# RWKV-7 inside a two-block fp32 network: the group norm's root and inverse on four columns per pair instead of 256, spread back through the tensor engine

## The reference, cut to what matters

```
y  = y - mean(y over the 64 channels of the head)
y  = y / sqrt(mean(y * y over the head) + 64e-5) * rw_lnx_g + rw_lnx_b
out = ((y + bonus) * gate) @ rw_wo
```

## Time and profile before

| | |
|---|---|
| median of 3 runs | 2728.96 us (2728.11 to 2732.6) |
| the profiled execution, its own time | 2738.52 us |
| its span, first to last instruction | 2737.0 us |
| busy, share of the span: PE, PEld, DVE, ACT, POOL | 96%, 84%, 76%, 59%, 8% |
| mean granted TensorE clock | 0.985 of full speed |
| the four RWKV units lie at | about 791 to 1004 us |
| the RWKV tail lies at | about 1004 to 1018 us |

### The profile page before, as it was taken

One profiled execution on the slowest core, in us unless ns is written; L12 is line 12 of the kernel. 1 busy time (PEld: TensorE's weight loads), 2 busy tenths in 40 slices (PEclk: granted clock), 3 DMA queues, 4 the chain that ended last, 5 costly groups with the idle time before them and its releaser, 6 DMA issues.

```text
span 2737.0 us, 43598 instructions
## 1 busy us (share of the span) xinstructions
PE 2635.5 (96%) x17668; PEld 2290.9 (84%) x17668; DVE 2068.2 (76%) x2973; ACT 1614.9 (59%) x2394; POOL 226.1 (8%) x229
## 2 busy tenths in 40 slices
PE   8999899999899999999999898999999999999997
PEld 7989789899787779998899896888888888888886
DVE  6667776776744557668655686999999999999995
ACT  5556455555332235543555535877787778778785
POOL 1102000000011117011600010000000000000000
PEclk9999999999999999999999999999999999999999
DMA  7553245455331125543355433999999999899992
GB/s 272 185 185 110 106 169 185 172 183 185 113 106 67 66 92 185 185 166 116 135 186 185 145 130 122 378 351 349 352 375 351 349 351 366 335 364 363 352 375 82
DMA packets 84605, 604.91 MB, mean 221 GB/s; under 512 B 9400, under 2 KB 9528, under 8 KB 12016
## 3 DMA queue, kind: packets, MB, share of 16 engines
q1 hardware_dynamic: 82016, 594.05, 58.9%
q10 hardware_dynamic: 2032, 4.85, 0.5%
q0 software_dynamic: 352, 3.15, 0.3%
HBM read 600.96 MB, written 1.05 MB: 220 GB/s over the span
## 4 chain that ended last, share of the span: by engine, by line
PE 88%; DVE 9%; ACT 2%; issue 1%; DMA 1%; ACTq 0%; DVEq 0%
PE bank L428 86%; DVE arena L2266 2%; DVE weights_lo L418 2%; PE bank L2856 1%; DVE arena L1200 1%; ACT weights_hi L410 1%; DVE rstd L479 1%; DMA x_T<-in_x 0%; DVE x_T L734 0%; DVE arena L2289 0%; DVE arena L555 0%; DVE arena L1202 0%; ACT x_T L546 0%; DVE arena L2980 0%; PE bank L1869 0%
## 5 line engine op out<-in xcount | busy, mean ns | idle before, releaser
L418 DVE TENSOR_TENSOR weights_lo<-raw_weights,weights_hi 128x1024 fp32r<-128x1024 f32 x816 | 1004.1, 1249 | 389.5 <-ACT weights_hi L410 383.9
L410 ACT CAST weights_hi<-raw_weights 128x1024 fp32r<-128x1024 f32 x816 | 849.5, 1050 | 333.4 <-PE bank L428 319.1
L428 PE MATMUL bank<-source,weights_hi 128*128 128x512 f32 (+1 forms) x3040 | 876.7, 356 | 43.0 <-DVE weights_lo L418 18.2
L428 PE MATMUL bank<-source,weights_lo 128*128 128x256 f32 x2400 | 682.2, 284 | 0.0
L428 PEld LDWEIGHTS bank<-source,weights_hi 128*128 128x128 f32 x3040 | 541.8, 194 | 130.6 <-issue 28.0
L428 PEld LDWEIGHTS bank<-source,weights_lo 128*128 128x128 f32 x2400 | 463.2, 193 | 0.1
L418 DVE TENSOR_TENSOR weights_lo<-arena,weights_hi 128x1024 fp32r<-128x1024 f32 x278 | 336.5, 1225 | 32.0 <-ACT weights_hi L410 28.5
L410 ACT CAST weights_hi<-arena 128x1024 fp32r<-128x1024 f32 x278 | 292.2, 1053 | 56.5 <-PE bank L428 40.3
L428 PE MATMUL bank<-weights_hi,source 128*128 128x512 f32 (+1 forms) x1024 | 309.6, 386 | 3.4 <-issue 2.8
L428 PE MATMUL bank<-hidden_hi,weights_hi 128*128 128x256 f32 x912 | 258.3, 283 | 0.0
L428 PE MATMUL bank<-hidden_lo,weights_hi 128*128 128x256 f32 x912 | 258.1, 283 | 0.0
(11 more groups left out here) (317 smaller groups left out, 3387.0 us busy)
## 6 DMA issues: line engine op xcount, KB each, us to landing
raw_weights<-in_exp_in SPq DMA_DIRECT2D x134, 1024.0 KB, 5.4
arena<-in_exp_in SPq DMA_DIRECT2D x90, 1024.0 KB, 5.4
raw_weights<-in_exp_w SPq DMA_DIRECT2D x67, 1024.0 KB, 5.3
arena<-in_exp_w SPq DMA_DIRECT2D x45, 1024.0 KB, 5.6
raw_weights<-in_ffn_w_down SPq DMA_DIRECT2D x44, 1024.0 KB, 5.0
raw_weights<-in_ffn_w_up SPq DMA_DIRECT2D x43, 1024.0 KB, 5.0
raw_weights<-in_ffn_w_gate SPq DMA_DIRECT2D x42, 1024.0 KB, 4.9
raw_weights<-in_dense_w SPq DMA_DIRECT2D x33, 1024.0 KB, 4.9
```

The costliest lines, as they stand in the source:

```text
L410: k.act.copy(k.weights(j)[0], raw_half(k, j)).then_inc(k.w_hi_ready, 1)
L418: k.dve.tensor_tensor(lo, raw_half(k, j), hi.bitcast(F32), ALU.subtract).then_inc(k.w_ready, 1)
L428: return k.pe.matmul(dst, lhsT, rhs, start=start, stop=stop, skip_group_check=shared)
```

## The change

The second head sum no longer fills 128 x 256 with every head's sum repeated over its 64 channels. The squares become the stationary operand, and two columns of `head_ones` the moving one, so that the sum comes out by tokens: 128 tokens x 2 heads, for two token tiles, four columns per pair. The root and the reciprocal work on these four columns. VectorE copies the inverse over 64 columns each into `z.y2` (128 x 256, tokens on the partitions), and TensorE turns it back into channels by tokens with products of `z.y2` and the identity (`spread_tensor`: two per slot, four per unit). The scaling reads the result from PSUM. `spread` becomes a use of banks 4 to 7 for units 0 to 2, and the finish of a unit has one step more: reciprocal and copy at round 2, nothing at 4, scaling at 6, bonus at 8, gate at 10.

```diff
@@ RwkvTiles
+        self.group = [[k.arena[:, at + 8 * i + 4 * j:at + 8 * i + 4 * (j + 1)] for j in range(2)] for i in range(PAIRS)]
@@ the list of bank uses
 for _u in range(1, UNITS):
-    RW_USES += [("K", _u), ("bonus", _u - 1), ("turn", _u - 1)] + [("gate", _c) for _c in range(4) if _u == 1]
+    RW_USES += [("K", _u), ("bonus", _u - 1), ("turn", _u - 1)]
+    RW_USES += [("gate", _c) for _c in range(4)] if _u == 1 else [("spread", _u - 2)]
     RW_USES += [("R", _u), ("norm", _u), ("inv", _u), ("V", _u)]
-RW_USES += [("bonus", UNITS - 1), ("turn", UNITS - 1)] + [("wo", _u) for _u in range(4)]
+RW_USES += [("bonus", UNITS - 1), ("turn", UNITS - 1), ("spread", UNITS - 2)] + [("wo", _u) for _u in range(4)]
+SPREAD_AFTER, SPREAD_ROUND, LAST_SPREAD_AFTER = 12, 5, 7
@@ claim_bank
+        elif earlier[0] == "spread":
+            k.pe.wait_ge(*k.pair_fin[PAIRS - 1].at((PAIRS * earlier[1] + PAIRS - 1, "y_scaled")))
@@ new
+def spread_bank(k, p, slot):
+
+    if p == UNITS - 1:
+        return k.bank[2 * slot + 1][:, 0:T]
+    return use_bank(k, ("spread", p))[:, slot * T:(slot + 1) * T]
+
+
+def spread_tensor(k, t, p):
+
+    if p < UNITS - 1:
+        claim_bank(k, ("spread", p))
+    for i in range(PAIRS):
+        z = PairTiles(k, t, PAIRS * p + i, i)
+        k.pe.wait_ge(*k.pair_fin[i].at((z.kt, "spread")))
+        for s in range(TT):
+            ins = mm(k, spread_bank(k, p, i)[:, s * P:(s + 1) * P], z.y2[:, s * P:(s + 1) * P], k.con("ident"), True, True)
+    ins.then_inc(*k.rw_mm.step(("spread", p)))
@@ dense_tensor
     if u < UNITS:
+        if p > 0:
+            yield from steps(keys, SPREAD_AFTER - 4)
+            spread_tensor(k, t, p - 1)
+            yield
         yield from keys
...
     else:
-        for v in range(4):
-            yield from wo_tensor(k, t, v, range(0, KT - 2 * PAIRS))
+        first = wo_early_tensor(k, t)
+        yield from steps(first, LAST_SPREAD_AFTER)
+        spread_tensor(k, t, p - 1)
+        yield
+        yield from first
@@ rwkv_tensor
-            for _ in range(count + (4 if p == 0 and n in GATE_ROUNDS else 0)):
-                next(dense, None)
+            more = (4 if n in GATE_ROUNDS else 0) if p == 0 else (1 if n == SPREAD_ROUND else 0)
+            for _ in range(count + more):
+                next(dense)
...
     for blocks in (range(KT - 2 * PAIRS, KT - PAIRS), range(KT - PAIRS, KT)):
         for v in range(4):
             for _ in wo_tensor(k, t, v, blocks):
                 pass
+            if v == 0 and KT - 1 not in blocks:
+                spread_tensor(k, t, UNITS - 1)
@@ pair_tensor
-    mm(k, b0[:, 0:T], head_ones, z.y2, True, True).then_inc(*p.step((kt, "sum2")))
+    for s in range(TT):
+        ins = mm(k, b0[:, 2 * s:2 * s + 2], z.y2[:, s * P:(s + 1) * P], head_ones[:, 0:P:HEAD], True, True)
+    ins.then_inc(*p.step((kt, "sum2")))
@@ pair_scalar
-    act.activation(z.y2, b0[:, 0:T], ACT.Sqrt, bias=k.con("eps_gn"), scale=1.0 / HEAD).then_inc(*a.step((kt, "std")))
+    act.activation(t.group[slot][0], b0[:, 0:4], ACT.Sqrt, bias=k.con("eps_gn"), scale=1.0 / HEAD)\
+        .then_inc(*a.step((kt, "std")))
@@ finish_vector
-    dve.reciprocal(z.y2, z.y2).then_inc(*d.step((kt, "rstd")))
+    root, inverse = t.group[slot]
+    dve.reciprocal(inverse, root).then_inc(*d.step((kt, "rstd")))
+    dve.wait_ge(*d.at((kt, "rstd")))
+    dve.tensor_copy(z.y2.rearrange("p (h c) -> p h c", h=4),
+                    inverse.rearrange("p (h o) -> p h o", o=1).to_broadcast([P, 4, HEAD])).then_inc(*d.step((kt, "spread")))
     yield
-    dve.wait_ge(*d.at((kt, "rstd")))
-    dve.scalar_tensor_tensor(z.y, z.y, k.col("rw_lnx_g", kt), z.y2, ALU.mult, ALU.mult).then_inc(*d.step((kt, "y_scaled")))
+    yield
+    dve.wait_ge(*k.rw_mm.at(("spread", kt // PAIRS)))
+    dve.scalar_tensor_tensor(z.y, z.y, k.col("rw_lnx_g", kt), spread_bank(k, kt // PAIRS, slot), ALU.mult, ALU.mult)\
+        .then_inc(*d.step((kt, "y_scaled")))
     yield
```

More of the change, by code:

```diff
@@ L1297, in __init__ @@
         self.root, self.inverse = k.arena[:, at:at + 8], k.arena[:, at + 8:at + 16]
+        at += 16
+        self.group = [[k.arena[:, at + 8 * i + 4 * j:at + 8 * i + 4 * (j + 1)] for j in range(2)] for i in range(PAIRS)]
         self.masks = k.arena[:, ARENA - N_RW_MASK * RW_CHUNK:ARENA]
@@ L1432, in wo_tensor, with wo_early_tensor @@
             yield
+def wo_early_tensor(k, t):
+    for v in range(4):
+        yield from wo_tensor(k, t, v, range(0, KT - 2 * PAIRS))
 def dense_tensor(k, t, p):
@@ L1502, in rwkv_tensor @@
                 next(pair)
-            for _ in range(count + (4 if p == 0 and n in GATE_ROUNDS else 0)):
-                next(dense, None)
+            more = (4 if n in GATE_ROUNDS else 0) if p == 0 else (1 if n == SPREAD_ROUND else 0)
+            for _ in range(count + more):
+                next(dense)
+        assert next(dense, None) is None
     for blocks in (range(KT - 2 * PAIRS, KT - PAIRS), range(KT - PAIRS, KT)):
@@ L1722, in rwkv_vector @@
         pairs = [pair_vector(k, t, PAIRS * p + i, i) for i in range(PAIRS)]
-        for n in range(ROUNDS + 4):
+        for n in range(ROUNDS + 6):
             for pair in pairs:
```

## The result

| | before | after |
|---|---|---|
| median of 22 runs each | 2734.68 us | 2739.53 us |
| lowest and highest | 2727.89, 2740.68 | 2732.53, 2753.38 |
| mean of the 22 | 2734.40 us | 2740.97 us |
| profiled execution: time, span, mean granted clock | 2738.52, 2737.0, 0.985 | 2735.93, 2734.5, 0.987 |

The ratio is 1.0023 with a 95% interval of 1.0013 to 1.0034: slower, by 6.3 us. No change lies outside the interval, while the 0.2% that the prediction took as the least that can be told lies inside it. The medians lie 4.9 us apart, the means 6.6. The means lie further apart because 6 of the 22 runs of the changed kernel lie at 2745.8 us or above, and of the 116 runs of the kernel before that were timed in all for this study none does (the highest is 2744.58). The profiled execution of the changed kernel is shorter than that of before, so two spans say nothing here; the rows have to.

What follows compares the result with a forecast made beforehand. TensorE, busy 96% of the span, was taken as the bound. Terms 3.8 + 0.2 + 2.3 - 1.2 = +5.1 us (+3.8 with the last unit at full clock), middle +4.5 on 2728.96, gave 2733.5 us, range 2728 to 2739.

Steps and rivals of the forecast that it cites:

- The base: Whole-kernel time of 2728.96 us, median of the runs shown, to which the +4.5 us was added.
- Spreading products: Four 128x128 TensorE products per unit, 0.95 us each four, hidden by no standstill: +3.8 us over four units.
- Reciprocals and head sum: Narrow reciprocals free VectorE in round 2, -0.60 us at each of two places; head sums cost +0.2 us over eight pairs.
- Reciprocals, the last unit at full clock: Last unit: x could start earlier after narrow reciprocals, another -1.3 us at full clock, nothing at the recorded half clock.
- Rival (b): Terms alone exceed the bound: spreading 0.98, waits 1.25, nothing won in last unit; +5.4, about 2735 us, slower; chance 0.15.
- Half clock in the last unit: Granted clock 0.50 for 10.2 us after the 1.65 us standstill in the last unit, costing 5.1 us.
- The head sum gives nothing back: Second head sum, two columns instead of 256, saves TensorE nothing: 0.46 against 0.43 us per slot; an instruction floor alone would save 2.7.
- The bank of R: Round 8, p = 1 and 2: R takes K's bank and waits for ScalarE's copy, 1.15 us each, +2.3 us.
- Waits on VectorE: Scaling in round 6 and gates moved to round 10 fit into VectorE's idle time; cost nothing.
- The bounds: Range for the summed terms of the whole change: +2.6 to +5.6 us.
- a slower kernel, by the clock: The 1.2 us standstill at R may trigger half clock, giving +6.2 to +9.6, 2735 to 2739 us; chance 0.17.

Runs made afterwards that it cites:

- e4: The changed kernel with R's bank as before and every spreading product issued twice; 2737.99 us, ratio 1.0021 to the kernel before.
- e1: The changed kernel with `spread` listed ahead of K, so R no longer takes K's bank; 2734.97 us, ratio 1.0000 to the kernel before.
- e3: The changed kernel with R's bank as before and no spreading products, scaling reading `z.y2` by tokens; 2735.98 us, ratio 1.0013 to the kernel before.
- e8: The kernel before with six extra 128x256 products at the start of the last `wo` stretch; 2740.20 us, ratio 1.0012.
- e5: The changed kernel run again unedited, for a second profile; 2740.86 us, ratio 1.0017 to the kernel before.
- e11: The changed kernel with ScalarE's copy of K in round 7 instead of 8, bank order kept; 2737.25 us, ratio 1.0006 to the kernel before.
- e10: The kernel before with more dense matmuls drawn into round 1 of the last unit, covering TensorE's 1.65 us wait; 2735.44 us, ratio 1.0004.
- e2: The kernel before with an empty bank use that makes R wait for the copy of K; 2741.43 us, ratio 1.0032.
- e6: The kernel before with two extra 128x256 products at the start of the last `wo` stretch (its series: 2, 4, 6); 2737.11 us, ratio 1.0002.
- e9: The changed kernel with R's bank as before and more dense matmuls in round 1 of the last unit; 2734.17 us, ratio 0.9999 to before.

## Why the prediction was wrong

The step that failed is the base. The change itself was priced at +4.5 us and the medians lie 4.9 apart; what put 2739.53 beyond the range is the number that the +4.5 was added to. Of the 6.0 us between 2733.5 and 2739.53 the base is 5.7, the change the small rest.

**The base.** "I take the middle, +4.5, on 2728.96" hung the range on the median of three runs. 22 runs have 2734.68, which is 5.7 us more. The text noted that the profiled execution lay 9.6 us above the three runs and still centred on them. Single executions spread over some 20 us, so three of them fix no base for a difference of 5. Moved by 5.7 us the range would have been 2733.7 to 2744.7. That the change alone came out so near is in part luck, as the terms show.

**The terms, one by one.** With the last unit at half clock the prediction had +5.1, and the distances give +5.0. With it at full clock it had +3.8, and the distances give 1.58 + 1.59 + 1.8 = +5.0 again.
- *Spreading products*, 3.8: measured 3.6 (e4 against e1).
- *Reciprocals and head sum*, two units: -1.2 + 0.1, measured -0.60 - 0.56 (e3). 2.30 to 1.69 us per place shows it in rows.
- *Reciprocals, the last unit at full clock*, -1.3: mis-sized. The wait of 1.35 us is there in e8, and without the spreading products removing it brings 1.0 (e3). But the changed kernel has none of that gain: e5 and e11 took 75.74 and 75.92 us from R to the end, 1.8 to 2.0 above the 73.9 of before at full clock, where 1.9 + 0.1 - 1.3 = 0.7 was forecast. Both have a pause inside a group of equal loads there (0.83 and 1.02 us), which e3, e8 and e10 lack; what makes it is open. Rival (b) had "nothing won in the last unit".
- *Half clock in the last unit*, 5.1: for the kernel as it stands 3.6, since at full clock another wait or pause comes back (77.48 beside 73.9, 79.32 beside 75.74).
- *The head sum gives nothing back*: 0.44 us beside 0.43. The 2.7 us that the prediction named as a possible saving didn't come; the row of the key norm decided rightly.
- *The bank of R*, 2.3: measured 2.5 (1.26 to 1.28 at each of two places, in after against e1 and in e2 against before). The text worked out 1.2 and counted 1.15 for fear of overlap; nothing overlapped.
- *Waits on VectorE*, nothing: right, but by less. The copies took 0.61 and 0.50 us, above the bound of 0.43 from the 512-wide copy. It changed nothing, since VectorE then idles 0.75 us.
- *The bounds*, "+2.6 to +5.6": the terms as bounded in the text add up to +3.1 to +5.4.

**The clock.** The rival "a slower kernel, by the clock", at 0.17, was kept apart as if it were a yes or no for the kernel. It is a yes or no for each execution: e5's profile shows it at R, and the first profile of the same kernel doesn't. So it belongs into the sum as an expected value. With the prediction's own numbers, 0.17 at each of two places and 5.1 us a time, it adds 1.7 us to the mean. The means differ by 6.6 us, 1.6 more than the +5.0 of the distances, but with an error of 1.5. It moved the mean if anything, and not the median. 7 of 33 runs of the changed kernel stand above 2745 us, and none of the 116 of before, none of e1's 12 and none of e11's 12, which lack the wait (they also lack its 2.5 us). That those seven runs owe their time to the wait at R is argued from this alone: e5's profiled execution, the only one seen with half clock behind R, took 2744.73 us and isn't one of them, and none of e2's 7 runs, which have the wait, lies above 2743.94.

**Against the rivals of the explanation.** That the spreading products make the difference to before: they cost 3.6 us, yet e1, which keeps them, equals before. That displacement in time makes it: e6 to e8 don't show it. That the order of the banks makes it: e11 keeps it and has no wait. The wait at R explains the direction in e1, e2 and e11, but by the distances only 2.5 us of the 4.6, 7.3 and 2.3 us that the medians moved (7.0, 8.0 and 4.2 by the means); the 2.3 is as it should be, the others aren't.

**What stays open.** Where the clock puts the rest. e1 and e9 have clock parts 1.7 and 3.3 us below that of before, and e3 has one 4.7 above it, with errors near 1, though none of the three has the wait at R. Each profile has half clock at some dozen places outside the mixer too, and these kernels change more than one pause. The balance "e1 equals before" thus holds by +2.5 us of distances and -2.5 in the rest of the mean, and only the first is understood. e2 is the other way round: +2.5 of distances and +5.5 in the rest, while in its one profile neither standstill at R is followed by half clock.

## What to carry to other kernels

When an operation gets a buffer from a rotating list, look up who gets which buffer behind it: here the place of the new entry in the list put an unrelated projection behind a copy that had not yet begun. Listed ahead of K it does no harm. On an engine that is 96% busy, price a new standstill at its length and, if it is longer than those known to be harmless, add the chance of losing the clock times what that costs. Measure a change of a few us as the distance between two instructions that both kernels have, on either side of it, where the clock is the same: single profiles here agreed to 0.1 us, while whole runs of one kernel lay 20 apart. And hang a forecast on a median only after asking how far single executions lie apart: if they differ by 10 us, three of them don't give a base for a difference of 5.

## What the runs showed of the hardware that was not expected

**VectorE's copy is slow beside GpSimd.** The same 128x256 copy takes 0.61 and 0.50 us in units 1 to 3 and 0.29 in the tail. The timelines of POOL, and of DVE in the tail, of the changed kernel:

```profile
906.50 0.75 POOL L2123 TENSOR_TENSOR weights_hi_scratch<-weights_hi_scratch,arena 128x256 f32<-128x256 f32 x1 [0.45 <-PE bank L428]
907.21 0.66 POOL L2128 TENSOR_TENSOR arena<-arena 128x256 f32<-128x256 f32 x1
...
1005.20 0.29 DVE L2100 COPY weights_hi_scratch<-arena 128x256 f32<-128x256 f32 x1 [0.21 <-DVE arena L2098]
```

The copy from 906.78 ends at 907.39, the GpSimd instruction that began before it at 907.25; the copy from 907.52 ends at 908.02, the next GpSimd instruction at 907.87. In the tail GpSimd has nothing to do. The Trainium skill ("SBUF — State Buffer", the entry on the shared port pair) says that the two engines share a pair of ports, for some of VectorE's operations, which one holds for its whole instruction while the other stands. The trace agrees in that each copy ends 0.14 to 0.15 us after the GpSimd instruction it met; that is less than the 0.29 that the copy takes alone, so it can't have stood for the whole of that instruction. The copies in the tail are the only ones without GpSimd's work beside them, and no run takes that work away in units 1 to 3, so the cause is read and not shown. The bound of 0.43 came from a copy at a place where GpSimd is idle.

**Half clock can last long behind a short pause.** 1.25 us of idle time were followed by 20.4 us at 0.50 (e5), 1.65 us by 10.2 us (7 of the first 10 profiles), both in stretches of 64x64 products with dense ones between, in which TensorE is busy without a break; and the same pause in another execution by none. In e8 even 1.65 and 1.35 us close together, and in e10 0.81 and 1.79, were followed by full clock.

**Pauses inside a group of equal loads.** Where the changed kernel and its relatives come to this place in the last unit at full clock, PEld pauses in the middle of 16 equal loads, with no releaser: 0.83 us in e5, 1.49 us in e9 (above, where the clock falls in the pause), and in e11

```profile
969.59 0.30 PEld L428 LDWEIGHTS bank<-arena,weights_lo_scratch 64*64 64x64 f32 x6 [1.02 <-issue]
```

It is absent from the profiles of e3, e8 and e10 at the same place. It stands where the gain of the narrow reciprocals at full clock is missing; what it is, these runs don't tell.
